# Modulation weights in one float32 product over four column strips, in buffers of their own

## The chip, the cores and the metric

One core of a Trainium2 chip runs the whole program. The metric is the device time of one execution in microseconds, the median of three runs. The core's engines work side by side and meet at semaphores: TensorE (PE, matmuls, and PEld for its weight loads), VectorE (DVE), ScalarE (ACT), GpSimd (POOL), and SyncE (SP), which here does nothing but issue transfers from the chip's memory (HBM) into the on-chip memory (SBUF). Matmul results go to PSUM, eight banks, here held as four pairs `PS[:, pair, half]`.

## The reference, cut to what matters

Two decoder layers run on 512 prompt tokens and 8 sample tokens. Each sub-layer is modulated by nine vectors per layer that come from a conditioning vector `c`, one row for the prompt and one for each of the 8 samples, so 9 rows in all:

```python
mod = jax.nn.silu(c) @ mod_w + mod_b            # (9 rows) x 1024 @ 1024 x 9216
sh0, sc0, gt0, sh1, sc1, gt1, sh2, sc2, gt2 = jnp.split(mod[:, None, :], 9, axis=-1)
h = modulate(rmsnorm(x, norm_pre[0]), sh0, sc0)  # h * (1 + scale) + shift
x = x + 0.5 * gt0 * rmsnorm(swiglu(h, ffn1_in, ffn1_out), norm_post[0])
...                                              # mixing of tokens, with sh1, sc1, gt1
h = modulate(rmsnorm(x, norm_pre[2]), sh2, sc2)
x = x + 0.5 * gt2 * rmsnorm(swiglu(h, ffn2_in, ffn2_out), norm_post[2])
```

`swiglu` multiplies by 1024 x 5632 gate and up weights, then by 2816 x 1024. All data are float32.

## The kernel before, in words

**Weights** come through a ring of four slots, `stage` (512 KB each, 128 x 1024 float32), in one order that is numbered through: a chunk's slot is its number modulo 4. ScalarE rounds a chunk to `w_hi` (L863), VectorE subtracts to get `w_lo` (`lo_apart` or `lo_over`, L1975), and TensorE multiplies `w_hi` and the rest with split activations, `h_hi` and `h_lo`: three products for each block. SP may load a chunk when the one four before it has been split (`lo_done`, L693).

**The gate loop** (`ffn_in`) makes 2 of 22 pairs of gate and up tiles a trip. With m = 0, 1 for the pair and gu = 0, 1 for gate and up, a trip is four tiles of TensorE, each 8 blocks x 3 products x 2 halves of 260 tokens. ScalarE takes `sil` from the gate tile (L949), VectorE multiplies it with the up tile to `hidf` (L2127), ScalarE rounds that to `hid_hi` (L955), VectorE makes `hid_lo`.

**The modulation rows** are a product of 1024 x 9216 a layer, cut into 18 groups of 512 columns. `c_st` holds `silu(c)` transposed, as 9 rounded columns and 9 of the rest; a chunk of weights is the moving operand. Eight groups of layer 0 are made in an opening, ahead of all else (`mod_pair`, 32 chunks, two groups at a time). The other 10, and all 18 of layer 1, are made **beside the gates**: a trip with `group` set has 8 chunks in place of 4, a gate or up chunk and a modulation chunk in turn (`per == 8`), and after each tile TensorE does one modulation chunk (`mod_rows`, 4 matmuls of 512 columns into pair 3). At the next trip, after the first tile, the rows are turned to columns by small matmuls (`turn_rows`), and VectorE adds the bias and writes `modT` (L2109). These trips are in six segments: `f1j0` and `f1i1` in layer 0 (5 trips each), `f2j0` and `f2i1` in layer 0 for layer 1's rows (5 each), and `f1j0` (5) and `f1i1` (3) in layer 1.

**PSUM in such a trip.** Since pair 3 is taken by the modulation rows, the fourth tile (m = gu = 1) goes into pair 0, as the first does:

```python
                                elif m == gu == 0 and per == 8:
                                    if not (type(i) is int and i == 0):
                                        pe.wait_ge(ev_d, i * 2 + ed)
                                    pair = 0
```

`ev_d` counts VectorE's `hidf` products, two a trip, so this wait of the first tile is for all products of the trip before.

Every engine executes its own list in order; a wait holds all that stands behind it on that engine. Nothing reorders the lists: they are as the code writes them.

## Time and profile before

| | |
|---|---|
| median of 3 runs | 3013.66 us (3008.25 to 3019.26) |
| profiled execution, span from first to last instruction | 3023.3 us |
| TensorE busy | 96% of the span |
| VectorE, ScalarE, GpSimd busy | 56%, 39%, 12% |
| mean granted TensorE clock | 0.974 |
| loaded by SP's queue | 296.60 MB |

The page gives the profiled execution by its span alone. Times in rows are microseconds from the span's start. A busy share is an average over stages; which engine sets the pace is read from each stage. A row with x2 or x8 is that many instructions of one kind merged, so its length is from the first one's start to the last one's end; matmuls overlap, so the distance of starts is what one costs. A float32 matmul shows as two records.

### The profile page before, as it was taken

What the parts mean: (1) busy time and instruction counts of PE and PEld (TensorE: products, weight loads), DVE (VectorE), ACT (ScalarE), POOL (GpSimd) and SP (SyncE); (2) the same over time, 40 slices, a digit from 0 to 9 for tenths busy, and PEclk for the clock granted to TensorE, in tenths of its full rate; (3) what the DMA queues carried; (4) which work ended last, traced back from release to release, by engine and by line L of the source; (5) the groups of instructions that cost most, each with busy time, mean ns of one, the idle gap of its engine ahead of it and who ended that gap; (6) DMA issues with size and microseconds to landing.
All of it is one profiled execution on the core that took longest, in us unless ns stands there. A gap on an engine that the chain in (4) does not pass through costs nothing.

```text
span 3023.3 us, 55792 instructions
## 1 busy us (share of the span) xinstructions
PE 2908.2 (96%) x22056; PEld 2703.3 (89%) x22056; DVE 1687.8 (56%) x3427; ACT 1193.3 (39%) x2023; POOL 366.7 (12%) x426
## 2 busy tenths in 40 slices
PE   6999999999999999999999999999999999999998
PEld 5899999899776689999999999999987767999997
DVE  5443346888869475424474424378878775632234
ACT  6533333545444244323334323245453532522222
POOL 2100000324025100000010000011330431100000
PEclk8999999999999999999999999999999999999998
DMA  7443443412224334434434434232222243232321
GB/s 265 127 153 98 141 147 91 137 50 64 57 75 124 107 98 124 145 101 153 124 93 133 141 100 149 86 109 99 57 64 62 62 133 119 85 97 82 100 76 64
DMA packets 448405, 324.28 MB, mean 107 GB/s; under 512 B 25114, under 2 KB 403346, under 8 KB 447451
## 3 DMA queue, kind: packets, MB, share of 16 engines
q1 hardware_dynamic: 442810, 296.60, 32.6%
q0 software_dynamic: 5408, 25.17, 2.5%
q8 instruction: 121, 1.98, 0.3%
q14 instruction: 66, 0.53, 0.1%
HBM read 310.48 MB, written 11.24 MB: 106 GB/s over the span
## 4 chain that ended last, share of the span: by engine, by line
PE 77%; DVE 15%; issue 3%; ACT 2%; DMA 1%; POOL 0%; another core or an unknown queue 0%; ACTq 0%; SPq 0%; DVEq 0%; POOLq 0%
PE PS L1306 77%; DVE score L2514 1%; DVE lo_over L1975 1%; DVE best L2513 1%; DMA stage<-in_mod_w 1%; DVE W L2444 1%; PE PS L1538 1%; DVE score L2504 1%; DVE xT L2071 1%; DMA stage<-in_w_branch_attn 1%; DVE counting L2251 0%; DVE sm L2197 0%; DVE tmpn L2069 0%; DVE lg L2680 0%; DVE dgr L2690 0%
## 5 line engine op out<-in xcount | busy, mean ns | idle before, releaser
L1306 PE MATMUL PS<-h_hi,w_hi 128*128 128x260 f32 (+1 forms) x4000 | 830.4, 289 | 10.5 <-POOL h_lo L2897 5.8
L1306 PE MATMUL PS<-h_lo,w_hi 128*128 128x260 f32 (+1 forms) x4000 | 808.0, 284 | 0.0
L1975 DVE TENSOR_TENSOR lo_apart<-stage,w_hi 128x1024 fp32r<-128x1024 f32 (+2 forms) x448 | 492.9, 1134 | 466.4 <-ACT w_hi L863 462.5
L1306 PEld LDWEIGHTS PS<-h_hi,w_hi 128*128 128x128 f32 (+1 forms) x4000 | 623.4, 189 | 60.5 <-issue 40.3
L1306 PEld LDWEIGHTS PS<-h_lo,w_hi 128*128 128x128 f32 (+1 forms) x4000 | 618.9, 189 | 0.0
L1306 PE MATMUL PS<-h_hi,lo_apart 128*128 128x260 f32 x2816 | 567.2, 283 | 0.0
L863 ACT ACTIVATE w_hi<-stage 128x1024 fp32r<-128x1024 f32 (+3 forms) x586 | 540.9, 954 | 46.8 <-DMA stage<-in_mod_w 15.3
L1306 PEld LDWEIGHTS PS<-h_hi,lo_apart 128*128 128x128 f32 x2816 | 434.6, 189 | 0.0
L1306 PE MATMUL PS<-hid_lo,w_hi 128*128 128x260 f32 x1408 | 283.8, 283 | 0.0
L1306 PE MATMUL PS<-hid_hi,w_hi 128*128 128x260 f32 x1408 | 283.2, 282 | 0.0
L1306 PE MATMUL PS<-hid_hi,lo_apart 128*128 128x260 f32 x1408 | 282.9, 282 | 0.0
L2127 DVE TENSOR_TENSOR hidf<-sil,PS 128x520 f32<-128x520 f32 x88 | 61.3, 697 | 366.5 <-PE PS L1306 366.5
L1306 PE MATMUL PS<-h_hi,lo_over 128*128 128x260 f32 (+1 forms) x1184 | 241.1, 286 | 0.0
L955 ACT ACTIVATE hid_hi<-hidf 128x520 fp32r<-128x520 f32 (+1 forms) x88 | 56.3, 639 | 450.9 <-DVE hidf L2127 450.9
L2878 POOL TENSOR_TENSOR hs<-yT,r_s 128x64 f32<-128x64 f32 x6 | 1.9, 320 | 1853.5 <-ACT r_s L929 1853.5
L1306 PEld LDWEIGHTS PS<-hid_hi,lo_apart 128*128 128x128 f32 x1408 | 217.0, 188 | 0.0
L1306 PEld LDWEIGHTS PS<-hid_hi,w_hi 128*128 128x128 f32 x1408 | 216.8, 188 | 0.1
L1306 PEld LDWEIGHTS PS<-hid_lo,w_hi 128*128 128x128 f32 x1408 | 216.7, 188 | 0.0
L1306 PEld LDWEIGHTS PS<-h_hi,lo_over 128*128 128x128 f32 (+1 forms) x1184 | 184.8, 190 | 0.0
L1975 DVE TENSOR_TENSOR lo_over<-stage,w_hi 128x1024 fp32r<-128x1024 f32 (+1 forms) x138 | 147.2, 1069 | 23.6 <-ACT w_hi L863 22.0
L949 ACT ACTIVATE sil<-PS 128x520 f32<-128x520 f32 x88 | 53.2, 604 | 263.2 <-PE PS L1306 263.2
L1306 PE MATMUL PS<-w_hi,c_st 128*128 128x512 f32 x288 | 116.5, 424 | 11.8 <-DVE lo_apart L1975 11.4
(436 smaller groups left out, 4088.6 us busy)
## 6 DMA issues: line engine op xcount, KB each, us to landing
stage<-in_ffn_in SPq DMA_DIRECT2D x176, 512.0 KB
stage<-in_mod_w SPq DMA_DIRECT2D x144, 512.0 KB
stage<-in_w_in SPq DMA_DIRECT2D x72, 512.0 KB
stage<-in_ffn_out SPq DMA_DIRECT2D x64, 384.0 KB
stage<-in_ffn_out SPq DMA_DIRECT2D x64, 320.0 KB
stage<-in_w_out SPq DMA_DIRECT2D x16, 512.0 KB
x_hold<-xT SPq DMA_DIRECT2D x2, 2080.0 KB
xT<-x_hold SPq DMA_DIRECT2D x2, 2080.0 KB, 8.1
```

Of the source, the lines that this page charges most:

```text
L863: nc.scalar.activation(w_hi[:, ch.slot, 0:ch.elems], stage[:, ch.slot, 0:ch.elems], ACT.Copy)\
L949: nc.scalar.activation(sil[:, m, :].rearrange("p (a n) -> p a n", a=2), PS[:, 2 * m, :, 0:HALF], ACT.Silu).then_inc(ev_a, 1)
L955: nc.scalar.activation(hid_hi[:, bass.ds(i * 2 + (s.first_tile + m), 1), :], hidf[:, m:m + 1, :], ACT.Copy)\
L1306: return nc.tensor.matmul(out, lhsT, rhs, start=start, stop=stop)
L1538: return nc.tensor.transpose(out, in_, ident[p0:p0 + size, p0:p0 + size])
L1975: nc.vector.tensor_tensor(lows(ch)[:, ch.slot, 0:ch.elems], stage[:, ch.slot, 0:ch.elems], w_hi[:, ch.slot, 0:ch.elems].bitcast(FP32), ALU ...
L2071: nc.vector.tensor_tensor(xT[:, k, 0:T], xT[:, k, 0:T], tmpn[:, k % 2, 0:T], ALU.add).then_inc(x_ready, 1)
L2127: nc.vector.tensor_tensor(hidf[:, m, :].rearrange("p (a n) -> p a n", a=2), sil[:, m, :].rearrange("p (a n) -> p a n", a=2), PS[:, up, :, ...
L2444: own(nc.vector.tensor_tensor_scan(W4[:, r, q, 1:NCH + 1], V(6)[:, g:g + 1].to_broadcast([P, NCH]), W4[:, r, q, 1:NCH + 1], 0.0, ALU.mult, ...
L2504: i = nc.vector.scalar_tensor_tensor(sc, rl[:, n % 2, 0:(t + 1) * P], wT[:, t, h:h + 1], sc, ALU.mult, ALU.add)
L2513: own.step(nc.vector.max(best[:], sc))
L2514: own.step(nc.vector.match_replace(sc, best[:], sc, TAKEN))
```

## The change

The modulation weights are no longer split. The whole float32 chunk is the moving operand of a float32 matmul whose stationary operand is `c32`, 32 columns of which 9 are used. A chunk of 1024 columns' worth is cut into four pieces of 256, and the four products go to four strips of 32 partitions of one PSUM bank. The chunks leave the ring: in the opening they go through `mod_open`, 8 slots that lie over `stage` and `w_hi`; beside the gates through four buffers `mod_stage`, one for each quarter of a group. A trip's four modulation chunks are all multiplied at its end, behind the fourth tile. The code can also make two groups a trip (`rate`), but every segment leaves `rate` at 1. ScalarE's list changes with it: what it splits in a trip is the four gate and up chunks alone, in the order of the trips without modulation. `scales` for the first post-norm moves behind the first feed-forward loop.

```diff
-    MOD_FIRST = GROUPS - (FT // 2 - 1)
+    MOD_FIRST = 8
     MOD_PAIRS = MOD_FIRST // 2
-    assert MOD_FIRST == 2 * MOD_PAIRS
+    FIRST_BESIDE = GROUPS - MOD_FIRST
...
-            self.group, self.of_layer, self.mods_before = group, of_layer, mods_before
-            self.per = 4 if group is None else 8
+            self.group, self.of_layer, self.mods_before, self.rate = group, of_layer, mods_before, rate
...
-        return [(s.phase, 4 * s.trips * (s.per // 4), BLK, 2 * s.trips, 2 * s.trips) for s in segments]
+        return [(s.phase, 4 * s.trips, BLK, 2 * s.trips, 2 * s.trips) for s in segments]
...
-    c_st = sb("c_st", [P, KD, P], FP32R)
+    c_st = sb("c_st", [P, 4, P], FP32R)
+    c32 = sb("c32", [P, KD, 32])
...
+    OPEN = 8
+    OPENED = KD * MOD_PAIRS
+    assert OPENED % OPEN == 0
+    mod_open = over("mod_open", [P, OPEN, BLK], ring0)
...
+    MOD_SLOTS = 4
+    mod_at = [arena0 + 2 * TOK * 4 + q * BLK * 4 for q in range(MOD_SLOTS - 1)] + [ffn.at]
+    assert mod_at[-2] + BLK * 4 <= norm_end and ffn.at + BLK * 4 <= nc.sbuf_usable_end
+    mod_stage = [over(f"mod_stage{q}", [P, BLK], at) for q, at in enumerate(mod_at)]
...
-                    for g in range(MOD_PAIRS):
-                        for k in range(4 if g == 0 else 0, KD):
-                            load(chunk('mod', k, g, 8), mod_weights(g, k).unsqueeze(1))
+                    for n in range(4, KD * MOD_PAIRS):
+                        if n >= OPEN:
+                            sp.wait_ge(mod_used, n - OPEN + 1)
+                        sp.dma_start(mod_open[:, n % OPEN, :], mod_weights(n // KD, n % KD)).then_inc(open_full[n % OPEN], 16)
+
+                def mod_load(s, i, m, j):
+
+                    sp.wait_ge(mod_used, i * (4 * s.rate) + (OPENED + 4 * (s.mods_before + m) + j - 3))
+                    sp.dma_start(mod_stage[j][:].rearrange("p (k n) -> p k n", k=2),
+                                 rows_of('mod_w', 2 * j, 2, i * (512 * s.rate) + (s.group + m) * 512, 512, bass.ds(s.of_layer, 1)))\
+                        .then_inc(mod_full[j], 16)
 
                 def ffn_in(s, name, f0):
-                    phase, per = s.phase, s.per
+                    phase = s.phase
 
                     def pair(i):
                         for j in range(4):
-                            load(chunk(phase, j * per // 4, i, per),
+                            load(chunk(phase, j, i, 4),
                                  rows_of(name, 0, KD, (j % 2) * DFF + (f0 + s.first_tile + i * 2 + j // 2) * P, P))
-                            if per == 8:
-                                load(chunk(phase, 2 * j + 1, i, per),
-                                     rows_of('mod_w', 2 * j, 2, i * 512 + s.group * 512, 512, bass.ds(s.of_layer, 1)))
+                            if s.group is not None:
+                                if type(i) is int and i == j == 0 and phase in ('f1j0', 'f2j0'):
+                                    sp.wait_ge(h_lo_ready, (N + (1 if phase == 'f1j0' else 3)) * KD)
+                                if s.rate == 1:
+                                    mod_load(s, i, 0, j)
+                                else:
+                                    mod_load(s, i, j // 2, 2 * (j % 2))
+                                    mod_load(s, i, j // 2, 2 * (j % 2) + 1)
...
                     def body(i):
                         for m in range(2):
-                            at = per // 2 * m
                             if m or split_here(phase, i):
-                                split(chunk(phase, at + 2, i, per))
-                            split(chunk(phase, at + 3, i, per))
-                            act.wait_ge(chunk_used, chunk(phase, at, i, per).number(1))
+                                split(chunk(phase, 2 * m + 2, i, 4))
+                            split(chunk(phase, 2 * m + 3, i, 4))
+                            act.wait_ge(chunk_used, chunk(phase, 2 * m, i, 4).number(1))
                             act.wait_ge(ev_d, i * 2 + (ed + m - 1))
                             nc.scalar.activation(sil[:, m, :].rearrange("p (a n) -> p a n", a=2),
                                                  PS[:, 2 * m, :, 0:HALF], ACT.Silu).then_inc(ev_a, 1)
-                            if per == 8:
-                                split(chunk(phase, at + 4, i, per))
-                                split(chunk(phase, at + 5, i, per))
                             act.wait_ge(ev_d, i * 2 + (ed + m + 1))
                             nc.scalar.activation(hid_hi[:, bass.ds(i * 2 + (s.first_tile + m), 1), :], hidf[:, m:m + 1, :], ACT.Copy)\
                                 .then_inc(hid_hi_ready, 1)
-                        if per == 8:
-                            act.wait_ge(chunk_used, chunk(phase, 7, i, per).number(1))
-                            act.wait_ge(rows_turned, i + (MOD_PAIRS + s.mods_before))
-                            nc.scalar.activation(modrow[:], PS[0:2 * NC, 3, 0, :], ACT.Copy).then_inc(rows_copied, 1)
+                            if s.group is not None and (m == 1 or s.rate == 2):
+                                n = m if s.rate == 2 else 0
+                                act.wait_ge(mod_used, i * (4 * s.rate) + (OPENED + 4 * (s.mods_before + n) + 4))
+                                act.wait_ge(rows_turned, i * s.rate + (MOD_PAIRS + s.mods_before + n))
+                                nc.scalar.activation(modrow[:], PS[:, 3, 0, 0:256], ACT.Copy).then_inc(rows_copied, 1)
...
-                def mod_rows(pair, ch, j):
-
-                    pe.wait_ge(lo_done, ch.number(1))
-                    for k in range(2):
-                        for w in (w_hi, lows(ch)):
-                            last = mm(PS[:, pair, 0, :], c_st[:, 2 * j + k, :], w[:, ch.slot, k * 512:(k + 1) * 512],
-                                      start=(j == 0 and k == 0 and w is w_hi), stop=(j == 3 and k == 1 and w is not w_hi))
-                    last.then_inc(chunk_used, 1)
+                def mod_rows(s, i, m, j):
+
+                    pe.wait_ge(mod_full[j], i * (16 * s.rate) + 16 * (OPENED // OPEN + s.mods_before + m + 1))
+                    for q in range(4):
+                        odd, half = q // 2, q % 2
+                        last = mm(PS[32 * q:32 * q + 32, 3, 0, 0:256], c32[:, 2 * j + odd, :],
+                                  mod_stage[j][:, odd * 512 + half * 256:odd * 512 + half * 256 + 256],
+                                  start=(j == 0), stop=(j == 3))
+                    last.then_inc(mod_used, 1)
 
                 def turn_rows(pair):
 
-                    for q in range(4):
-                        last = mm(PS[:, pair, 1, q * NC:(q + 1) * NC], modrow[:, q * P:(q + 1) * P], sel18[:])
+                    by_block = PS[:, pair, 1, 0:4 * NC].rearrange("p (h q c) -> p q h c", h=2, q=2)
+                    for q in range(2):
+                        last = mm(by_block[:, q], modrow[:, q * P:(q + 1) * P], halves_sel[:].rearrange("p (h c) -> p h c", c=NC))
                     last.then_inc(rows_turned, 1)
...
-                        ch = chunk('mod', k, g, 8)
-                        pe.wait_ge(lo_done, ch.number(1))
+                        n = KD * g + k
+                        pe.wait_ge(open_full[n % OPEN], 16 * (n // OPEN + 1))
                         if k == 0 and g >= 2:
                             pe.wait_ge(ev_a, g - 1)
-                        for w in (w_hi, lows(ch)):
-                            for half in range(2):
-                                last = mm(PS[:, 2 * (g % 2), half, :], c_st[:, k, :], w[:, ch.slot, half * 512:(half + 1) * 512],
-                                          start=(k == 0 and w is w_hi), stop=(k == KD - 1 and w is not w_hi))
-                        last.then_inc(chunk_used, 1)
+                        for q in range(4):
+                            last = mm(PS[32 * q:32 * q + 32, 2 * (g % 2), 0, 0:256], c32[:, k, :],
+                                      mod_open[:, n % OPEN, q * 256:(q + 1) * 256], start=(k == 0), stop=(k == KD - 1))
+                        last.then_inc(mod_used, 1)
...
-                                if m == gu == 0 and per == 8 and not (type(i) is int and i == 0):
-                                    turn_beside(i)
-                                if per == 8:
-                                    mod_rows(3, chunk(phase, 4 * m + 2 * gu + 1, i, per), 2 * m + gu)
+                                if gu == 0 and beside and (m and s.rate == 2 or not m and not (type(i) is int and i == 0)):
+                                    turn_beside(i, m)
+                                if gu == 1 and beside and (m or s.rate == 2):
+                                    for j in range(4):
+                                        mod_rows(s, i, m if s.rate == 2 else 0, j)
...
-                    for k in range(KD):
-                        split(chunk('mod', k + 2, g, 8))
-                        if k == 4 and g:
-                            pair_added(g - 1)
...
-                            at = per // 2 * m
                             if m or split_here(phase, i):
-                                split(chunk(phase, at + 2, i, per))
-                            split(chunk(phase, at + 3, i, per))
-                            if m == 1 and per == 8 and not (type(i) is int and i == 0):
+                                split(chunk(phase, 2 * m + 2, i, 4))
+                            split(chunk(phase, 2 * m + 3, i, 4))
+                            if m == 1 and first_group is not None and not (type(i) is int and i == 0):
                                 rows_beside(i)
                             dve.wait_ge(ev_a, i * 2 + (ea + m + 1))
-                            if per == 8:
-                                split(chunk(phase, at + 4, i, per))
-                                split(chunk(phase, at + 5, i, per))
-                            dve.wait_ge(chunk_used, chunk(phase, at + per // 4, i, per).number(1))
-                            up = 0 if m == 1 and per == 8 else 2 * m + 1
+                            dve.wait_ge(chunk_used, chunk(phase, 2 * m + 1, i, 4).number(1))
+                            up = 0 if m == 1 and first_group is not None else 2 * m + 1
...
```

**SyncE's list**, inside the loop of segment `f1j0` of layer 0, a trip's first three loads. ISA and REGISTER_ALU rows carry the waits in a loop. Before, gate (`in_ffn_in`) and modulation (`in_mod_w`) loads into one ring:

```order
L693 ISA [waits lo_done]
L693 DMA stage<-in_ffn_in 128x8x128
L691 REGISTER_ALU
L693 ISA [waits lo_done]
L693 DMA stage<-in_mod_w 128x2x512
L691 REGISTER_ALU
L693 ISA [waits lo_done]
L693 DMA stage<-in_ffn_in 128x8x128
```

And now:

```order
L714 ISA [waits lo_done]
L714 DMA stage_64<-in_ffn1_in 128x8x128
L726 REGISTER_ALU
L727 ISA [waits mod_used]
L727 DMA mod_stage0_84<-in_mod_w 128x2x512
L710 REGISTER_ALU
L714 ISA [waits lo_done]
L714 DMA stage_64<-in_ffn1_in 128x8x128
```

The modulation load stands where it stood, between two gate loads, but waits for TensorE's use of the buffer (`mod_used`) and no longer for a split.

**ScalarE's list**, same loop, the second half of a trip (m = 1) around `sil`. Before, it splits the fourth gate chunk and the fourth modulation chunk of the trip (slots 2 and 3), does `sil`, and splits the next trip's first two:

```order
L862 REGISTER_ALU [waits stage_full2]
L863 ACTIVATE w_hi<-stage 128x1024 [waits chunk_used]
L862 REGISTER_ALU [waits stage_full3]
L863 ACTIVATE w_hi<-stage 128x1024 [waits chunk_used]
L947 REGISTER_ALU
L948 REGISTER_ALU [waits chunk_used]
L949 ACTIVATE sil<-PS 128x520 [waits ev_d]
L860 REGISTER_ALU
L863 ACTIVATE w_hi<-stage 128x1024 [waits chunk_used,stage_full0]
```

And now, where slots 0 and 1 are gate chunks 0 and 1 of the next trip:

```order
L894 REGISTER_ALU
L899 ACTIVATE w_hi<-stage 128x1024 [waits chunk_used,stage_full0]
L896 REGISTER_ALU [waits stage_full1]
L899 ACTIVATE w_hi<-stage 128x1024 [waits chunk_used]
L980 REGISTER_ALU
L981 REGISTER_ALU [waits chunk_used]
L982 ACTIVATE sil<-PS 128x520 [waits ev_d]
L984 REGISTER_ALU
```

Both splits of the next trip's chunks now stand ahead of `sil`.

**TensorE's list** where one trip of that segment ends and the next begins. Before, the fourth modulation chunk, then the loop and the wait of its first tile:

```order
L1306 MATMUL PS<-w_hi,c_st 128x512 [waits lo_done]
L1306 MATMUL PS<-lo_apart,c_st 128x512
L1306 MATMUL PS<-w_hi,c_st 128x512
L1306 MATMUL PS<-lo_apart,c_st 128x512
L644 UNCONDITIONAL_BRANCH
L644 ISA
L1422 ISA [waits ev_d]
```

And now all four chunks, in strips of 32 partitions:

```order
L1337 MATMUL PS<-mod_stage_84,c 32x256 [waits mod_full0]
L1337 MATMUL PS<-mod_stage_84,c 32x256 x3
L1337 MATMUL PS<-mod_stage_85,c 32x256 [waits mod_full1]
L1337 MATMUL PS<-mod_stage_85,c 32x256 x3
L1337 MATMUL PS<-mod_stage_86,c 32x256 [waits mod_full2]
L1337 MATMUL PS<-mod_stage_86,c 32x256 x3
L1337 MATMUL PS<-mod_stage_87,c 32x256 [waits mod_full3]
L1337 MATMUL PS<-mod_stage_87,c 32x256 x3
L659 UNCONDITIONAL_BRANCH
L659 ISA
L1454 ISA [waits ev_d]
```

The wait for `ev_d` has stayed; 16 strip matmuls stand ahead of it where 4 wide ones stood, and the other 12 wide ones have gone from between the tiles.

## Rows read from the trace of the kernel before

**Rows 1.** The page: the span, and the chain by line.
```profile
span 3023.3 us, 55792 instructions
...
PE PS L1306 77%; DVE score L2514 1%; DVE lo_over L1975 1%; DVE best L2513 1%; DMA stage<-in_mod_w 1%; DVE W L2444 1%; PE PS L1538 1%; DVE score L2504 1%; DVE xT L2071 1%; DMA stage<-in_w_branch_attn 1%; DVE counting L2251 0%; DVE sm L2197 0%; DVE tmpn L2069 0%; DVE lg L2680 0%; DVE dgr L2690 0%
```

**Rows 2.** TensorE in order of time: start, length, line, operation, out<-in.
```profile
121.10 0.39 PE L1306 MATMUL PS<-w_hi,c_st 128*128 128x512 f32 x1
...
122.02 0.40 PE L1306 MATMUL PS<-h_hi,w_hi 128*128 128x260 f32 x2
...
127.78 0.39 PE L1306 MATMUL PS<-w_hi,c_st 128*128 128x512 f32 x1
```

**Rows 3.** TensorE in order of time, at and after a trip's end.
```profile
141.14 0.39 PE L1306 MATMUL PS<-w_hi,c_st 128*128 128x512 f32 x1
...
142.17 0.51 PE L1306 MATMUL PS<-h_hi,w_hi 128*128 128x260 f32 x2
...
148.13 1.05 PE L1306 MATMUL PS<-sel,modrow 18*128 18x9 f32 x8
```

**Rows 4.** One trip: length, busy PE, PEld, DVE, ACT, POOL, clock, DMA.
```profile
142.74:170.85 28.11, 28.11 (x218) 26.97 (x217) 12.44 (x13) 10.55 (x14) 0.00 (x0) 1.00 0.48 149
```

**Rows 5.** The tile modT: minimum, median, maximum in ns.
```profile
L2109 DVE TENSOR_TENSOR modT<-PS,vecT x28: 186/189/197, 160.8 to 1902.3; 128x36 f32 x15, 128x36 f32<-128x36 f32 x13
```

**Rows 6.** VectorE in order of time, same trips.
```profile
122.95 1.23 DVE L1975 TENSOR_TENSOR lo_apart<-stage,w_hi 128x1024 fp32r<-128x1024 f32 x1 [2.64 <-ACT w_hi L863]
...
141.34 0.69 DVE L2127 TENSOR_TENSOR hidf<-sil,PS 128x520 f32<-128x520 f32 x1 [2.66 <-PE PS L1306]
```

**Rows 7.** The opening in order of time, engines mixed; idle time ahead in brackets.
```profile
20.89 47.25 SPq L693 DMA_DIRECT2D stage<-in_mod_w  x28
20.92 1.22 PE L1306 MATMUL PS<-w_hi,c_st 128*128 128x512 f32 x2 [3.64 <-DVE lo_apart L1975]
...
24.44 1.06 ACT L863 ACTIVATE w_hi<-stage 128x1024 fp32r<-128x1024 f32 x1 [1.46 <-DMA stage<-in_mod_w]
...
80.00 1.28 ACT L919 ACT_TABLE_LOAD   x1
...
82.98 0.27 ACT L919 ACTIVATE std<-PS,eps 128x5 f32<-128x5 f32 x1 [1.69 <-PE PS L1306]
...
92.14 0.59 PE L1306 MATMUL PS<-h_hi,w_hi 128*128 128x260 f32 x2
```

**Rows 8.** Two stretches of loads, the columns of rows 4, GB/s last.
```profile
5.00:7.90 2.90, 0.00 (x0) 0.00 (x0) 0.00 (x0) 0.00 (x0) 2.06 (x8) 1.00 1.02 414
...
72.00:80.00 8.00, 6.20 (x24) 4.69 (x23) 5.05 (x5) 5.55 (x6) 1.82 (x1) 0.78 0.96 281
```

**Rows 9.** TensorE in order of time, float32 of 512 columns.
```profile
1014.19 3.60 PE L1306 MATMUL PS<-kv,Exd 128*64 128x512 f32 x8
1017.72 0.39 PE L1306 MATMUL PS<-y_hi,w_hi 128*128 128x260 f32 x1
```

**Rows 10.** TensorE in order of time, float32 in strips of 32 columns.
```profile
724.80 0.39 PE L1306 MATMUL PS<-h_hi,lo_over 128*128 128x260 f32 x2
725.12 0.67 PE L1306 MATMUL PS<-CA,BXl 128*32 128x128 f32 x16
725.72 0.50 PE L1306 MATMUL PS<-h_hi,w_hi 128*128 128x260 f32 x2
```

**Rows 11.** A gate load's issue, and the split that uses it.
```profile
70.27 0.38 SPq L693 DMA_DIRECT2D stage<-in_ffn_in  x1
...
75.58 1.06 ACT L863 ACTIVATE w_hi<-stage 128x1024 fp32r<-128x1024 f32 x1 [1.43 <-DMA stage<-in_ffn_in]
```

**Rows 12.** Stretches after TensorE has waited, the columns of rows 4.
```profile
20.90:24.30 3.40, 3.38 (x8) 2.71 (x9) 3.37 (x3) 2.08 (x3) 1.26 (x1) 0.50 0.68 206
...
2613.10:2618.40 5.30, 5.30 (x16) 4.43 (x17) 5.13 (x8) 3.94 (x6) 3.52 (x3) 0.50 0.00 0
```

More of the change, by code:

```diff
@@ L64, in arrivals @@
     def arrivals(self):
-        n = 16 * (self.base // 4 + 1)
+        n = 16 * (self.base // 4 + 1) + self.before
         return n if self.shift is None else self.shift * 4 + n
@@ L450, in build @@
     vec_in = sem("vec_in")
+    mod_full = [sem(f"mod_full{q}") for q in range(MOD_SLOTS)]
+    mod_used = sem("mod_used")
+    open_full = stage_full + mod_full
     def mod_weights(g, k):
@@ L481, in _ @@
         def _(pool):
-            own = Chain(pool, pool_own)
+            own = Chain(pool, pool_step)
             def pick_where(t, value, pattern, base, mult, op, fill):
@@ L493, in _ @@
             pick_where(ident[:], ident[:], [[-1, P]], 0, 1, ALU.not_equal, 1.0)
[L494 to L495 removed]
+            by_half = halves_sel[:].rearrange("p (h c) -> p h c", c=NC)
+            for odd in range(2):
+                pick_where(by_half, by_half, [[-32, 2], [-1, NC]], -64 * odd, 1, ALU.not_equal, 1.0)
             by_sample = samesample[:].rearrange("p (b g) -> p b g", g=NPG)
@@ L515, in _ @@
             pool.memset(r_s[:], 1.0).then_inc(consts_ready, 1)
+            own.wait()
+            steps_taken['pool'] = own.n
         @block.scalar
@@ L540, in _ @@
                                            ident[0:NC, 0:NC])
-            last.then_inc(c_turned, 1)
+            last.then_inc(x_turned, 1)
         @block.vector
         def _(dve):
-            own = Chain(dve, dve_own0)
+            own = Chain(dve, dve_own)
             dve.wait_ge(consts_ready, 1)
@@ L1332, in pair_turned @@
                         pe.wait_ge(ev_d, g - 1)
-                    for q in range(8):
-                        last = mm(PS[:, 1, g % 2, q * NC:(q + 1) * NC], modrows[:, q // 4, q % 4 * P:(q % 4 + 1) * P], sel18[:])
+                    for q in range(2):
+                        last = nc.tensor.transpose(PS[:, 1, g % 2, q * P:(q + 1) * P], modrows[:, g % 2, q * P:(q + 1) * P], ident[:])
                     last.then_inc(rows_turned, 1)
@@ L1442, in ffn_in @@
                 def ffn_in(s, j=None):
-                    phase, per = s.phase, s.per
+                    phase, beside = s.phase, s.group is not None
                     ea, ed = evicts_a[phase], evicts_d[phase]
@@ L1460, in body @@
                     def body(i, h_waits=None):
-                        if h_waits is not None and per == 4:
-                            tiles_together((0, 1, 2), [chunk(phase, q, i, per) for q in range(3)], (h_hi, h_lo), h_waits)
+                        if h_waits is not None:
+                            tiles_together((0, 1, 2), [chunk(phase, q, i, 4) for q in range(3)], (h_hi, h_lo), h_waits)
                         for m in range(2):
                             for gu in range(2):
-                                if h_waits is not None and per == 4 and 2 * m + gu < 3:
+                                if h_waits is not None and 2 * m + gu < 3:
                                     continue
-                                if m == gu == 1 and per == 8:
+                                if m == gu == 1 and beside:
                                     pe.wait_ge(ev_a, i * 2 + (ea + 1))
                                     pair = 0
-                                elif m == gu == 0 and per == 8:
+                                elif m == gu == 0 and beside:
                                     if not (type(i) is int and i == 0):
@@ L1480, in body @@
                                         pe.wait_ge(mod_added, mods_added(l))
-                                tile(pair, [(chunk(phase, (2 * m + gu) * per // 4, i, per), 0, KD, P)], (h_hi, h_lo),
+                                tile(pair, [(chunk(phase, 2 * m + gu, i, 4), 0, KD, P)], (h_hi, h_lo),
                                      h_waits=h_waits if m == gu == 0 else None)
@@ L1497, in ffn_in @@
                     each(pe, s.trips, trip, last=False)
-                    if per == 8:
+                    if beside:
                         turn_beside(s.trips)
@@ L1982, in pair_added, with scales @@
                     dve.wait_ge(rows_turned, g + 1)
[L1983 to L1994 removed]
+                    bias = vecT[:, 48 + 8 * g:56 + 8 * g].rearrange("p (j q) -> p q j", q=2)
+                    nc.vector.tensor_tensor(modT[:, 8 * g:8 * g + 8, :].rearrange("p (j q) c -> p q j c", q=2),
+                                            PS[:, 1, g % 2, 0:2 * P].rearrange("p (q j c) -> p q j c", q=2, j=4)[:, :, :, 0:NC],
+                                            bias.unsqueeze(3).to_broadcast([P, 2, 4, NC]), ALU.add).then_inc(ev_d, 1)
+                def scales(j, pre=True, post=True):
                     def blocks(which):
@@ L2134, in body @@
                                                     ALU.subtract).then_inc(hid_lo_ready, 1)
+                            if m == 1 and first_group is not None and s.rate == 2:
+                                rows_beside(i, 1)
                     each(dve, s.trips, body)
-                    if per == 8:
+                    if first_group is not None:
                         rows_beside(s.trips)
```

128 lines of the change are left out of this document (63 added, 65 removed).

## Prediction

> **What bounds the kernel now.** I read the page first: of a span of 3023.3 us the chain that ended last runs over TensorE's matmuls for 77% [rows 1]. A microsecond counts if TensorE works or stands in it.
>
> Next, TensorE in order of time inside a trip of the gate loop. A modulation chunk is four matmuls from 121.10 to 122.02, 0.92 us. The next stands at 127.78, 6.68 us after the first, so a gate or up tile takes 6.68 - 0.92 = 5.76 us (48 matmuls at 0.12), with no gap [rows 2]. A trip is four tiles and four chunks, 26.72 us, and the turn of the finished rows, which begins at 148.13 [rows 3]. Together it is 28.11 us: in the stretch 142.74 to 170.85, from one trip to the same place of the next, PE is busy for all of it at a granted clock of 1.00, VectorE for 12.44 and ScalarE for 10.55 us [rows 4]. In these loops only TensorE's work counts. There are 28 such trips (the sum for `modT` is made 28 times, rows 5), in segments of 5, 5, 5, 5, 5 and 3.
>
> The seam between trips needs care. The last tile of a trip goes into PSUM pair 0, and so does the first of the next, so TensorE must wait until VectorE has taken the product `hidf` out. Now that product starts at 141.34 and takes 0.69 us [rows 6] while TensorE is covered by the fourth modulation chunk, begun at 141.14; the next tile starts at 142.17, 1.03 us after the old one's end [rows 3].
>
> Last, the opening. TensorE waits for splits, these for transfers, and the first gate matmul is at 92.14. The 28 loads issued from 20.89 on take 47.25 us, 1.69 each [rows 7]; with nothing holding the queue back, 4 KB rows move at 414 GB/s (1.27 us a chunk of 512 KB), gate chunks at 281 (1.87 us) [rows 8].
>
> **The change, part by part.**
>
> *Matmuls beside the gates.* Removed: 4 chunks x 0.92 = 3.68 us a trip. Added: 16 products of 256 columns in float32. What float32 costs: eight records of 512 columns (four matmuls, two passes each) begin at 1014.19, and the next matmul at 1017.72, 0.43 us a record counting a step of shape [rows 9]; so 256 columns are 0.215 us a pass. Whether four column strips run at once: sixteen records of 128 columns, in strips of 32, occupy 725.12 to 725.72, 0.60 us; one after the other, at a quarter of 0.43, they would take 1.7. From the last full-width matmul (0.12 after 724.80) to the next full-width one it is 0.80 us; four rounds of 0.108 and a step of 0.12 leave 0.25 us for going in and out [rows 10]. So a trip's product is 4 chunks x 2 passes x 0.215 + 0.25 = 1.97 us; without overlap, its upper bound, 32 x 0.215 = 6.9 us.
> The Trainium skill (TensorEngine Tiling, Key Properties) says that changing the tiling mode drains TensorE. By that rule the trace's 0.25 us is paid at each change of shape, and the new code, with a trip's four chunks together, pays it once.
>
> *Turning the rows.* Now 8 records in 1.05 us [rows 3], some 0.11 us each; then 4: -0.45 us a trip.
>
> *The splits.* Four copies and four subtractions a trip vanish from ScalarE and VectorE. They lie under TensorE's work [rows 4]: no gain in itself.
>
> *The loads, and the new wait.* SP serves its list in order. Each modulation load now waits until TensorE has used the same buffer a trip earlier, and all four uses stand at the trip's end. Modulation load 0 stands ahead of gate chunk 1, so gate chunk 1 of trip i+1 is not asked for before TensorE has done all four tiles and the first modulation chunk of trip i. ScalarE, in the second half of trip i, splits gate chunks 0 and 1 of trip i+1 and only then does `sil` of that half; before, what stood ahead of `sil` had long been asked for. `hidf` waits for `sil`, and the next first tile for `hidf`. So **TensorE stands at each seam for a whole load.** Worked out from the last tile's end (141.14 in the old trip):
> - change of shape 0.12, first chunk 0.43, its end and the signal 0.15: SP is free at 0.70. Modulation load 0 leaves at 0.80, gate chunk 1 one issue later, 1.25.
> - the transfer: a gate chunk issued at 70.27 with another ahead of it is first used at 75.58, 5.3 us [rows 11]; so here at 6.55. Bounds from its issue: one chunk at 414 and one at 281 GB/s with some 0.5 us of start, 3.6; with one more of 1.87 sharing the queue and as much again for its neighbour, 7.
> - ScalarE's split 1.06 [rows 11]: 7.61. VectorE's split 1.23, the sum for `modT` 0.19 and the product 0.69 [rows 5, 6], with `sil` beside them: 9.72. TensorE starts 0.14 later, as now: 9.9 us against 1.03.
>
> TensorE's own 1.97 us lie inside these 9.9, so at such a seam the cheaper product gains nothing; TensorE is idle for 7.9 us. Late behind it is everything of the next trip, but once: chunks 2 and 3 have a tile or more to land.
>
> *The clock.* After a TensorE gap of 3.64 us (20.92, rows 7) the granted clock is 0.50, 1.2 GHz, over 20.90 to 24.30. In the second layer a stretch of 5.30 us with TensorE busy throughout, just after a wait for h_lo, is at 0.50 too [rows 12]. Half speed for 3.4 us loses about 1.5 us of matmul work (a little less than half of it), for 5.3 us 2.4. I take 1.5, the row whose gap I know, with 0 and 2.4 as bounds.
> The Trainium skill (TensorE: Matmul & The Clock Gate, "HAM oscillation — how this bites in real kernels") warns of this pattern, a loop that waits for data between bursts. By it every seam pays; without it the sum would be 33 us less.
>
> *How many seams.* The wait bites between trips of one segment: 4+4+4+4+4+2 = 22. In a segment's first trip the buffers have long been free, and after its last come loads with no such wait. Per seam +8.9 (9.9 - 1.03), -2.76 (the other three chunks), -0.45, +1.5 = +7.2; x22 = **+158 us**. The 6 last trips: -3.68 + 1.97 - 0.45 = -2.16; x6 = **-13 us**.
>
> *The opening.* The 28 loads now leave without splits, eight buffers deep. The first is used 3.5 us after its issue (20.89, 24.44, rows 7); issued at some 18.6: 22.1; 27 more at 1.27: 56.4. Gate chunk 2 lands at 56.4 + 3 x 1.87 = 62.0; split, table load and `std` (1.06, 1.28, 0.27) end at 64.7, where now they end at 83.25; the rest, 8.9 us to the first gate matmul, stays [rows 7]. So 73.6 for 92.14: **-18.5 us** (-12 if a chunk takes 1.5 us).
>
> Sum: +158 - 13 - 18.5 = +126.5 on the profiled 3023.3, so 3150. That execution is 9.6 us above the median of the three timed ones, 3013.66; set on the median, **3140 us**.
>
> **The rivals.**
> - *The seam is hidden.* Were gate chunk 1 there in time, each trip would gain 2.16: 28 x 2.16 + 18.5 = 79, **2935 us**. All else in the change shortens work. It decides at (13 + 18.5)/22 = 1.4 us net a seam, against 7.2: the chunk would have to land 5.8 us earlier, before it is asked for. What remains is that I misread what a wait counts. 0.08.
> - *The seam is cheaper.* Landing after 3.6 and no loss by the clock: 22 x 3.2 less, **3070 us**. The gap of 3.64 us that did lower the clock speaks against the second half. 0.12.
> - *The seam is dearer.* The queue, asked for eight chunks in a burst, lands chunk 1 after 7 us and the clock costs 2.4: 22 x 2.6 more, **3197 us**. 0.10.
> - *The strips do not overlap in this form.* The first chunk is then 1.3 us later at each seam (28 us), the last trips cost 6 x 4.9 and the opening some 12: **3209 us**. The sixteen records in 0.60 us speak against it. 0.05.
> - *Seam and gains cancel* within 0.3% (9 us, about what a measurement of this kernel can tell). It needs 1.0 to 1.8 us net a seam. 0.02.
> - The forecast, 3100 to 3175: 0.63.
>
> **How the numbers follow.** Slower by over 0.3% are the forecast, the cheap and the dear seam and the strips, 0.90; same 0.02; faster 0.08. The range, 3075 to 3190, takes in most of the cheap and the dear seam's cases and leaves out the hidden one and the separate strips.
>
> **What the profile after would show.** A TensorE gap of 7 to 8 us ahead of a first tile in 22 places, the matmuls behind it at clock 0.50; 28 bursts of 32 records in about 2 us; `sil` held up by a split that waits for a transfer; the issue of gate chunk 1 right behind the first modulation chunk's use; trips of some 35 us; the first gate matmul near 74. I am wrong if the seams are under 3 us, or if the strips' records come 0.2 us apart.

## The result

| | before | after |
|---|---|---|
| median | 3016.32 us (3008.25 to 3019.26, 4 runs) | 3153.97 us (3147.07 to 3165.95, 4 runs) |
| profiled execution, span | 3023.3 us | 3145.3 us |
| TensorE busy, mean granted clock | 96%, 0.974 | 91%, 0.949 |

The ratio is 1.047, 95% interval 1.044 to 1.050: the change makes the kernel 138 us slower by the medians. I predicted 3140 us, slower, with a range of 3075 to 3190.

**The page** of after, its span, its chain by line, and the group of the gate tiles' first product (count | busy us, mean ns | idle time ahead and what ended it), answers to [rows 1]:

```profile
span 3145.3 us, 56068 instructions
...
PE PS L1337 71%; DMA stage<-in_ffn_in 4%; DVE score L2542 1%; DVE lo_over L2008 1%; DVE best L2541 1%; DMA mod_open<-in_mod_w 1%; ACT w_hi L899 1%; DVE W L2472 1%; DVE score L2532 1%; DMA stage<-in_w_branch_attn 1%; DVE xT L2099 1%; DVE counting L2279 1%; PE PS L1571 0%; DMA stage<-in_w_in 0%; DVE tmpn L2097 0%
...
L1337 PE MATMUL PS<-h_hi,w_hi 128*128 128x260 f32 (+1 forms) x4000 | 851.4, 295 | 182.4 <-DVE hidf L2151 171.9
```

A transfer that is not among the chain's parts shown in [rows 1], the gate weights', is on it now with 4%, and TensorE's tiles stand 171.9 us waiting for `hidf`. The view of waits (us in total, times, longest) counts how often:

```profile
PE PS L1337 <- DVE hidf L2151: 171.9, 22, 9.0
...
SPq L727 <- PE PS L1337: 584.8, 22, 28.8
```

22 waits of TensorE, one for each place where two trips of a segment meet, and 22 waits of SP's queue at the modulation load (L727) for TensorE. The same number on both sides fits one cause but does not show it: e1 and e2 below keep the 22 waits of the queue (429.3 and 443.9 us in all) and lose TensorE's. One seam in order of time, TensorE first (start, length, then the idle time ahead in brackets):

```profile
228.53 0.41 PE L1337 MATMUL PS<-h_hi,lo_apart 128*128 128x260 f32 x2
228.87 1.93 PE L1337 MATMUL PS<-mod_stage,c 128*32 128x256 f32 x32
238.50 0.80 PE L1337 MATMUL PS<-h_hi,w_hi 128*128 128x260 f32 x2 [7.70 <-DVE hidf L2151]
```

SP's queue:

```profile
229.72 0.37 SPq L727 DMA_DIRECT2D mod_stage<-in_mod_w  x1
230.34 0.37 SPq L714 DMA_DIRECT2D stage<-in_ffn_in  x1
```

ScalarE and then VectorE:

```profile
235.34 1.06 ACT L899 ACTIVATE w_hi<-stage 128x1024 fp32r<-128x1024 f32 x1 [15.48 <-DMA stage<-in_ffn_in]
236.31 0.58 ACT L982 ACTIVATE sil<-PS 128x520 f32<-128x520 f32 x1
```
```profile
236.43 1.23 DVE L2008 TENSOR_TENSOR lo_apart<-stage,w_hi 128x1024 fp32r<-128x1024 f32 x1 [15.31 <-ACT w_hi L899]
237.57 0.19 DVE L2137 TENSOR_TENSOR modT<-PS,vecT 128x36 f32 x1
237.68 0.69 DVE L2151 TENSOR_TENSOR hidf<-sil,PS 128x520 f32<-128x520 f32 x1
```

Read it from the end. The tile at 238.50 follows the end of `hidf`. VectorE started `hidf` at 237.68, as soon as it had done the split of 236.43 and the small sum for `modT`. That split waited for ScalarE's, and ScalarE had waited 15.48 us for a transfer, the one issued at 230.34, right behind a modulation load that could go only when TensorE had used the first chunk of its burst. Before, the same seam took 1.03 us [rows 3].

What follows the seam is slow too. Windows of after (length, then busy time of PE, PEld, DVE, ACT and POOL, granted clock, DMA share, GB/s):

```profile
228.85:238.50 9.65, 1.95 (x34) 0.94 (x33) 1.94 (x3) 1.55 (x2) 0.00 (x0) 0.79 0.84 248
238.50:241.90 3.40, 3.40 (x15) 3.40 (x16) 1.93 (x2) 1.85 (x3) 0.00 (x0) 0.50 1.10 335
241.90:244.70 2.80, 2.80 (x15) 2.80 (x14) 1.23 (x1) 1.06 (x1) 0.00 (x0) 0.51 1.14 311
```

TensorE is busy throughout the second and third, but at a granted clock of 0.50 and 0.51, 1.2 GHz. By the Trainium skill (TensorE: Matmul & The Clock Gate, "HAM oscillation — how this bites in real kernels") a loop that waits for data between bursts pays so each time round; the trace agrees, in all 22 places.

From turn to turn of the rows, a trip with a seam in it now takes 35.42 us on the mean of 16, where it took 28.11 [rows 4]: +7.31. The last trips' interval takes 20.50 where it took 23.23: -2.73.

**The opening** got shorter. TensorE, ScalarE and TensorE again:

```profile
26.65 0.64 PE L1337 MATMUL PS<-mod_open,c 128*32 128x256 f32 x8 [0.64 <-DMA mod_open<-in_mod_w]
29.48 1.02 PE L1337 MATMUL PS<-mod_open,c 128*32 128x256 f32 x8 [2.19 <-DMA mod_open<-in_mod_w]
...
59.01 0.64 PE L1337 MATMUL PS<-mod_open,c 128*32 128x256 f32 x8 [0.72 <-DMA mod_open<-in_mod_w]
```
```profile
64.25 1.06 ACT L899 ACTIVATE w_hi<-stage 128x1024 fp32r<-128x1024 f32 x1 [0.68 <-DMA stage<-in_ffn_in]
...
66.62 0.27 ACT L953 ACTIVATE std<-PS,eps 128x5 f32<-128x5 f32 x1
```
```profile
75.78 0.64 PE L1337 MATMUL PS<-h_hi,w_hi 128*128 128x260 f32 x2
```

The first gate matmul is at 75.78 where it was at 92.14 [rows 7]: -16.4. In sum: 22 x 7.31 = +160.8, 6 x -2.73 = -16.4, the opening -16.4: +128.0. The two spans differ by +122.0. The other 6 us lie outside these trips: between the last turn of layer 0's second segment and the first of its third it is 726.37 us where it was 722.97, though it holds a seam of +7.31, so 3.9 less; behind the last turn of all the stretch is 3.8 shorter; from layer 0's last turn to layer 1's first it is 2.4 more than a seam accounts for. The same kernel run again takes 730.52 in the first of these stretches, 4.1 more than here, so differences of this size need no cause in the code.

### The profile page after: what moved, and what is told of

Same layout as the page of the kernel before. It is cut to its first block, busy times and chain, and to the rows that moved or that the text cites. A ratio compares the mean times of both kernels' runs of the same rounds, so it can differ in the third digit from the quotient of the medians.

```text
span 3145.3 us, 56068 instructions
## 1 busy us (share of the span) xinstructions
PE 2855.1 (91%) x22464; PEld 2647.6 (84%) x22464; DVE 1516.8 (48%) x3282; ACT 1047.4 (33%) x1879; POOL 360.4 (11%) x427
## 4 chain that ended last, share of the span: by engine, by line
PE 72%; DVE 15%; DMA 6%; issue 3%; ACT 3%; SPq 0%; POOL 0%; DVEq 0%; another core or an unknown queue 0%; ACTq 0%; POOLq 0%
PE PS L1337 71%; DMA stage<-in_ffn_in 4%; DVE score L2542 1%; DVE lo_over L2008 1%; DVE best L2541 1%; DMA mod_open<-in_mod_w 1%; ACT w_hi L899 1%; DVE W L2472 1%; DVE score L2532 1%; DMA stage<-in_w_branch_attn 1%; DVE xT L2099 1%; DVE counting L2279 1%; PE PS L1571 0%; DMA stage<-in_w_in 0%; DVE tmpn L2097 0%
## 5 line engine op out<-in xcount | busy, mean ns | idle before, releaser
L1337 PE MATMUL PS<-h_hi,w_hi 128*128 128x260 f32 (+1 forms) x4000 | 851.4, 295 | 182.4 <-DVE hidf L2151 171.9
L1337 PEld LDWEIGHTS PS<-h_hi,w_hi 128*128 128x128 f32 (+1 forms) x4000 | 635.7, 195 | 226.8 <-DVE lo_apart L2008 182.1
L1337 PE MATMUL PS<-h_lo,w_hi 128*128 128x260 f32 (+1 forms) x4000 | 823.0, 288 | 0.0
L1337 PEld LDWEIGHTS PS<-h_lo,w_hi 128*128 128x128 f32 (+1 forms) x4000 | 635.8, 194 | 0.0
L2008 DVE TENSOR_TENSOR lo_apart<-stage,w_hi 128x1024 fp32r<-128x1024 f32 (+2 forms) x304 | 321.5, 1085 | 625.5 <-ACT w_hi L899 621.9
L1337 PE MATMUL PS<-h_hi,lo_apart 128*128 128x260 f32 x2816 | 581.8, 289 | 0.0
L899 ACT ACTIVATE w_hi<-stage 128x1024 fp32r<-128x1024 f32 (+4 forms) x442 | 398.0, 923 | 407.3 <-DMA stage<-in_ffn_in 384.0
L1337 PEld LDWEIGHTS PS<-h_hi,lo_apart 128*128 128x128 f32 x2816 | 449.7, 195 | 0.0
L2157 DVE TENSOR_TENSOR hid_lo<-hidf,hid_hi 128x520 fp32r<-128x520 f32 (+1 forms) x88 | 61.6, 700 | 75.2 <-ACT hid_hi L985 75.2
```

Of the source, the lines that this page charges most:

```text
L899: nc.scalar.activation(w_hi[:, ch.slot, 0:ch.elems], stage[:, ch.slot, 0:ch.elems], ACT.Copy)\
L1337: return nc.tensor.matmul(out, lhsT, rhs, start=start, stop=stop)
L2008: nc.vector.tensor_tensor(lows(ch)[:, ch.slot, 0:ch.elems], stage[:, ch.slot, 0:ch.elems], w_hi[:, ch.slot, 0:ch.elems].bitcast(FP32), ALU ...
L2157: nc.vector.tensor_tensor(hid_lo[:, f, :], hidf[:, m:m + 1, :], hid_hi[:, f, :].bitcast(FP32), ALU.subtract).then_inc(hid_lo_ready, 1)
```

## The experiments

The kernels were timed in two sets, each beside the kernel before: e1 to e4 in the first, where that kernel's median was 3018.36 us, and e5 to e9 in the second, where it was 3015.20. The changed kernel, run again in the second set (**e9_after_again**), stands for the first set's as well.

> The changed kernel itself, unchanged, beside the others of this set, to put the prices of the filler and of the second load ahead on a firm base. 3154 again within 10 us; its profile shows 22 TensorE gaps of 7.5 to 9 us as before.

3148.35 us (3143.27 to 3158.73), ratio 1.044 (1.041 to 1.046); 22 waits of 175.5 us in all. The price of the change is 133 to 138 us.

### e1_swap: three loads moved by one place each

```diff
 for j in range(4):
     load(chunk(phase, j, i, 4),
...
-    if s.group is not None:
...
+    if s.group is not None and j > 0:
...
         if s.rate == 1:
-            mod_load(s, i, 0, j)
+            mod_load(s, i, 0, j - 1)
+            if j == 3:
+                mod_load(s, i, 0, 3)
```

Modulation loads 0, 1 and 2 each go behind one more gate load; load 3 stays last. Gate chunk 1 now has no modulation load ahead of it. The wait for `h_lo` that two segments have in their first trip moves with load 0.

> Each modulation load is issued one gate chunk later, so that gate chunk 1 of a trip no longer has one ahead of it. Theory (the seam is gate chunk 1's issue time and nothing else): all 22 TensorE gaps of 7.5 to 9 us go, a trip lasts 25.4 us from turn to turn, and the clock loss behind the gaps goes too; 28 x 2.7 + 16.4 = 93 us less than the kernel before's 3016, about 2925. Rival (the memory queue or the splits' own rate holds the chunk, not its place): gaps stay above 3 us, 3050 or more. Second rival (gate chunk 2, which now stands behind the wait, becomes the late one): a gap ahead of the second gate tile, over 2 us.

2928.92 us (2921.98 to 2937.82), ratio 0.971 (0.967 to 0.974): 219 to 225 us faster than the changed kernel, and faster than before. TensorE at the seam, and a window of one trip:

```profile
197.59 1.93 PE L1339 MATMUL PS<-mod_stage,c 128*32 128x256 f32 x32
199.46 0.51 PE L1339 MATMUL PS<-h_hi,w_hi 128*128 128x260 f32 x2
```
```profile
171.90:197.47 25.57, 25.57 (x230) 24.50 (x228) 7.71 (x9) 6.78 (x9) 0.00 (x0) 1.00 0.56 164
```

No gap is left and no half speed; every trip takes 25.57 us. The rival of a limit by the queue's or the splits' rate falls: the same bytes are loaded and split. So does the one of gate chunk 2 as the next late one. As this trip has no wait, it also prices the new work: from the last gate matmul to the next tile's first it is 2.08 us, of which 0.12 is a gate matmul, so a burst costs 1.96 us.

### e2_sil_first: the late chunk left late, sil ahead of its split

```diff
-split(chunk(phase, 2 * m + 3, i, 4))
+late = m == 1 and s.group is not None
+if not late:
+    split(chunk(phase, 2 * m + 3, i, 4))
...
 nc.scalar.activation(sil[:, m, :].rearrange("p (a n) -> p a n", a=2),
                      PS[:, 2 * m, :, 0:HALF], ACT.Silu).then_inc(ev_a, 1)
+if late:
+    split(chunk(phase, 2 * m + 3, i, 4))
```

VectorE's list has the same edit, with its split behind `hidf`.

> The loads keep their order, so gate chunk 1 is asked for as late as in the changed kernel; ScalarE and VectorE do sil and hidf of the trip's second half before they split that chunk. Theory (the first tile waits only because sil stands behind the split): the first tile starts some 1.6 to 2.2 us after the last one's end; the chunk is low and ready at 8.9, the second tile could start at about 8.4, so a wait of 0.5 to 1 us moves to there; about 2940. Rival (the late chunk costs its lateness wherever it is waited for): the gap of 7 us moves to the second tile, 3150.

2955.27 us (2952.16 to 2963.66), ratio 0.979 (0.976 to 0.982). The gap at the first tile is gone though the transfer comes as late as before, so what TensorE waited for was the order of ScalarE's and VectorE's lists. A trip takes 26.69 us on the mean, 1.1 more than in e1, and the rest sits behind the first tile, as expected. ScalarE, VectorE and TensorE in a trip whose seam is at 206:

```profile
211.23 1.06 ACT L899 ACTIVATE w_hi<-stage 128x1024 fp32r<-128x1024 f32 x1 [11.70 <-DMA stage<-in_ffn_in]
212.19 0.62 ACT L989 ACTIVATE hid_hi<-hidf 128x520 f32 x1
212.72 0.36 ACT L995 ACTIVATE modrow<-PS 128x256 f32<-128x256 f32 x1
```
```profile
212.32 1.23 DVE L2012 TENSOR_TENSOR lo_apart<-stage,w_hi 128x1024 fp32r<-128x1024 f32 x1 [6.95 <-ACT w_hi L899]
```
```profile
213.23 0.59 PE L1341 MATMUL PS<-halves_sel,modrow 128*128 128x18 f32 x4 [0.83 <-ACT modrow L995]
213.67 0.49 PE L1341 MATMUL PS<-h_hi,w_hi 128*128 128x260 f32 x2
```

The wait shows at the turn of the rows, ahead of the second tile, because the copy to `modrow` stands behind the late split: 14.0 us in 18 places. But the second tile had to wait for the chunk as well, as I expected. Its subtraction ends at 213.55 and the tile starts at 213.67, 0.12 us later; in the 22 trips that distance is 0.07 to 0.29 us. So the turn's wait lies inside the chunk's, and a copy that came sooner would have gained next to nothing. In the trip of 27.26 us the chunk's split began some 0.7 us later than in the others. In the two longest, 27.84 and 27.94 us, TensorE ran at half speed for 3.4 us, soon after waits of 1.45 and 1.55 us.

### e3_filler: the gap filled with useless matmuls

```diff
 if not (type(i) is int and i == 0):
+    pe.wait_ge(ev_d, i * 2 + (ed - 1))
+    kept_running(PS[:, 1, 0, :], 34)
     pe.wait_ge(ev_d, i * 2 + ed)
```

> The changed kernel with 34 matmuls of 512 columns of no use in each of the 22 gaps, into a free PSUM pair, before the wait for hidf. They take some 7.3 us of the 7.8 us gap. Theory (about 2 us of a seam's price is the lowered clock behind the gap): the granted clock stays at 1.00 across the seam, the first tile takes 5.7 us for 7.67, and the time falls by 22 x 2.0 = 44 us to about 3110. Rival (the first tile is long for another reason, such as the chunk's arrival): no change, 3154. If the filler runs past the gap, up to 22 x 0.5 us is added.

3098.16 us (3087.94 to 3110.21), ratio 1.025 (1.022 to 1.029), 50 to 56 us less than the changed kernel, with 748 more matmuls. Windows over a seam (the first from the burst to the next tile) and over that tile:

```profile
220.76:230.47 9.71, 9.71 (x68) 7.29 (x67) 1.93 (x3) 1.59 (x3) 0.00 (x0) 1.00 0.87 250
230.47:236.22 5.75, 5.75 (x49) 5.75 (x49) 3.15 (x3) 2.88 (x4) 0.00 (x0) 1.00 1.12 325
```

The seam is as long as ever, but the clock stays at 1.00, 2.4 GHz, and the first tile takes 5.75 us. In the changed kernel it takes 7.2 to 8.6 us in the 22 places, 7.8 on the mean. A trip takes 33.44 us, 2.0 less. 22 x 2.0 = 44 us is the clock's share. That is in keeping with the timed difference: beside the changed kernel of the other set, the ratios are 0.018 apart with some 0.004 of uncertainty, 43 to 67 us.

### e4_spread: strips, but one chunk behind each tile

```diff
-if gu == 1 and beside and (m or s.rate == 2):
-    for j in range(4):
-        mod_rows(s, i, m if s.rate == 2 else 0, j)
+if beside:
+    mod_rows(s, i, 0, 2 * m + gu)
```

> The modulation chunks in strips as in the changed kernel, but one behind each tile, where they stood before, the loads in the changed order. Modulation buffer 0 is then free after the first tile of a trip, three tiles earlier. Theory: no gap at the seam, since gate chunk 1 is asked for three tiles earlier; a trip pays the change of shape four times, 4 x (0.43 + 0.25) + 23.04 + 0.52 = 26.3 us for 28.11 before; 28 x 1.8 + 16.4 = 67 us less than before, about 2950. Rival (buffers of their own and not the burst at the end make the seam): gaps of over 5 us stay, 3100 or more.

2969.30 us (2961.34 to 2974.52), ratio 0.984 (0.981 to 0.987). The load order is that of the changed kernel and no long gap is left: the first modulation buffer is free three tiles earlier. So buffers of their own and the loads' order are not enough for a seam; it needs the burst at the trip's end as well. A trip takes 26.92 us where I had 26.3. Two chunks in order of time, the second at a trip's end:

```profile
198.90 0.64 PE L1337 MATMUL PS<-mod_stage,c 128*32 128x256 f32 x8
199.47 0.51 PE L1337 MATMUL PS<-h_hi,w_hi 128*128 128x260 f32 x2
...
205.43 0.64 PE L1337 MATMUL PS<-mod_stage,c 128*32 128x256 f32 x8
206.44 0.51 PE L1337 MATMUL PS<-h_hi,w_hi 128*128 128x260 f32 x2 [0.36 <-DVE hidf L2150]
```

The second is 1.01 us ahead of the next tile where the first is 0.57: one chunk is no longer enough to cover `hidf`. That is 0.44 of the 0.6 us by which the trip is longer than I had it; the rest I did not follow.

### e5_serial: e1's loads, all products in one column strip

```diff
-last = mm(PS[32 * q:32 * q + 32, 3, 0, 0:256], c32[:, 2 * j + odd, :],
+last = mm(PS[0:32, 3, 0, 0:256], c32[:, 2 * j + odd, :],
           mod_stage[j][:, odd * 512 + half * 256:odd * 512 + half * 256 + 256],
-          start=(j == 0), stop=(j == 3))
+          start=(j == q == 0), stop=(j == q == 3))
```

The opening's matmuls are changed in the same way.

> e1's order of loads, and all four products of a modulation chunk in column strip 0, one on top of the other (the rows come out wrong: the sum of four quarters), so that no two can run at once; the number of matmuls and their columns stay. Theory (four strips run at once, a round of four 256-column passes in 0.215 us): the burst of 32 records grows from 1.56 to some 6.7 us from first to last start, a trip from 25.57 to 30.7 us, the opening from 1.28 to 1.72 us a chunk; 28 x 5.1 + 14 = 157 us more than e1's 2929, about 3085. Rival (the strips gain little, the saving is that a product in float32 needs no second operand): burst unchanged within 1 us, 2930 to 2960.

3091.60 us (3087.57 to 3095.81), ratio 1.025 (1.023 to 1.027), 160 us more than e7, its neighbour in the set. TensorE:

```profile
361.11 7.09 PE L1339 MATMUL PS<-mod_stage,c 128*32 128x256 f32 x32
368.13 0.51 PE L1339 MATMUL PS<-h_hi,w_hi 128*128 128x260 f32 x2
```

The same 32 records now take 6.71 us from the first start to the last, for 1.55: a pass of 256 columns costs 6.71 / 31 = 0.22 us alone, and four in four strips cost 1.55 / 7 = 0.22 us together. A trip takes 30.73 us, and 28 x 5.16 = 144 us of the 160 are there, the rest in the opening (first gate matmul at 91.61 for 75.34 in e7). In float32 on one strip the product is dearer than the split one it replaced; all of its gain is the four strips.

### e8_two_ahead: one modulation load more ahead of gate chunks 1, 2 and 3

```diff
-    mod_load(s, i, 0, j)
+    for q in ((0, 1), (2,), (3,), ())[j]:
+        mod_load(s, i, 0, q)
```

> The changed kernel with two modulation loads ahead of gate chunk 1 of each trip, so that this chunk waits for the second modulation chunk's use and has one load more ahead of it in the queue. Theory (the seam is set by when gate chunk 1 lands): it is asked for 0.6 us later and lands 0.6 to 1.9 us later; seams of 10.6 to 11.9 us for 9.96, 22 x that difference = 13 to 41 us more than the changed kernel, 3167 to 3195. Rival (the seam is a fixed cost of meeting at pair 0, whatever the loads do): seams of 9.96 and no change.

3195.51 us (3193.60 to 3199.94), ratio 1.060 (1.059 to 1.062): 47 us more than the changed kernel beside it, a little over the range I gave. SP's queue and ScalarE, at a seam whose last gate matmul starts at 367.36:

```profile
368.55 1.01 SPq L727 DMA_DIRECT2D mod_stage<-in_mod_w  x2
369.81 0.37 SPq L714 DMA_DIRECT2D stage<-in_ffn_in  x1
```
```profile
375.69 1.06 ACT L900 ACTIVATE w_hi<-stage 128x1024 fp32r<-128x1024 f32 x1 [17.02 <-DMA stage<-in_ffn_in]
```

From issue to split it is now 5.9 us, where it was 5.0 (230.34 to 235.34): a load ahead costs its issue, 0.6, and here 0.9 more behind it in the queue. The seams are 11.92 us on the mean, 1.8 to 2.0 more than the changed kernel's. The seam is no fixed price of meeting at pair 0.

### e7_both: both cures

The edits of e1 and e2 together.

> Both cures together: each modulation load one gate chunk later (e1), and sil and hidf of a trip's second half ahead of the split of the next gate chunk (e2). Theory (with the chunk there in time, nothing waits for the splits either): trips of 25.57 us as in e1, the same time as e1 within the measurement, about 2929. Rival (the splits held sil up by a little in every trip, seen or not): seams under 2.08 us and up to 22 x 0.3 = 7 us less.

2931.17 us (2919.50 to 2939.16), ratio 0.972 (0.969 to 0.975): the same as e1, trips of 25.57 us. Either cure removes the seam; where the loads are in order, that of the lists brings nothing. The version that beats both kernels is e1.

## Why the prediction was right, and where its sizes were off

**Sign and mechanism** were right: "TensorE stands at each seam for a whole load". It is shown by e1 and e8, which change only the places of modulation loads in SP's list and take the seam away or lengthen it, and by e2, which leaves the load late and takes the wait for it out of `hidf`'s way.

**The seam.** Predicted 9.9 us from the last tile's end; measured 9.96 from the start of its last matmul, so 9.84. Its stations, from that end (228.77, 0.12 after the last gate matmul of the trip shown; forecast in brackets): modulation load 0.95 (0.80), gate chunk 1 issued 1.57 (1.25), ScalarE's split 6.57 (6.55), `hidf` from 8.91 (9.03 in the same sum), tile 9.73 (9.9). The transfer was 0.3 us shorter than the 5.3 of [rows 11] and the issues 0.3 later, which cancelled: that part of the agreement is luck.

**The clock** was the mis-sized term: 1.5 us a seam from [rows 12], 2.0 measured (the first tile takes 7.8 us on the mean for 5.75) and 2.0 by e3's trips. I took the half speed to last 3.4 us; it lies over 3.0 to 6.2 us of the first tile, 4.4 on the mean, and the seam shown above is one of the longest. Over 22 seams that is some 11 us more than forecast.

**The sum** hides it. It was forecast at +126.5 and came to +128.0 by the same terms: a seam's trip cost 7.31 for the 7.2 forecast, because the turn and the chunks that went gave back most of what the clock took more. So the clock is not why 3140 was 14 us low. The medians lie 137.7 us apart, 11 more than forecast, and the spans of the two profiled executions 122.0: the one before (3023.3) was longer than all four timed ones (3008.25 to 3019.26), the one after the shortest of its four. The other 2.7 us of the 14 are what the median before rose by with a fourth run.

**The new work** was right: 1.97 us a burst, measured 1.96, overlap and mode change included. By the Trainium skill (TensorEngine Tiling, Key Properties) a change of mode drains the array; e1 shows its size here, 1.96 - 8 x 0.215 = 0.24 us for going in and out.

**The turn** gave more than the 0.45 us I took: the next matmul stands 0.37 us behind its start (179.75, 180.12 in e1) for 0.99 before (148.13, 149.12), and the chunk behind it, which cost 1.03 and not 0.92, went too. With the 0.11 us more that the chunk at the seam cost, e1's trip comes out: -3.68 + 1.96 - 0.62 - 0.11 - 0.11 = -2.56, measured -2.54. The last trips' -2.73 for -2.16 has the same cause in the main.

**The opening** gave 16.4 us for 18.5. The chunks came every 1.28 us as forecast, but for one pause (26.65 to 29.48, some 1.5 us more), and the last was used at 59.0; the rest of the chain stayed as it was, as assumed (9.16 us from `std` to the first gate matmul in both). The term varies from run to run: in the profiles of the experiments, e5's aside, the first gate matmul is at 74.10 to 76.01.

**The rivals.** "The strips do not overlap" is refuted by e5. "The seam is hidden" did not happen, but its 2935 us is about what e1 reached (2929) by the places of three loads: the gain was real, and it was in the new work, not in the order around it. "Dearer" is about what e8 made, 3196 for 3197 us, though with a transfer of 5.9 us where that rival had 7: the agreement of the two times is partly chance. That taking away the splits gains nothing in itself I read from [rows 4] and did not try.

## What to carry to other kernels

Ask of each wait in a queue what stands behind it, not what it guards: here the wait for a buffer whose data was not needed before the next trip's end held up a load that was needed at once. When uses are gathered into a burst, their buffers come free in a burst too, and late; then put the loads for them behind those that are wanted sooner. A gap on TensorE can cost more than its length: here 2.0 us of lost speed on top of 7.8 us of idling.

## What the runs showed of the hardware

- Four float32 products of 256 columns in four column strips took the time of one, 0.22 us a pass; in one strip each took its own (e5 against e1).
- The half speed after the gaps of 7.5 to 9.0 us lay over 3.0 to 6.2 us of the tile behind, from seam to seam; after the gap of 3.64 us in [rows 7, 12] it lasted 3.4. The length of the one gap just before does not settle whether the clock falls. After a gap of 2.12 us in e2 it stayed at 1.00 over the next 6.8 us, and after one of 1.45 us it fell (TensorE, then windows):

```profile
1157.02 0.59 PE L1341 MATMUL PS<-halves_sel,modrow 128*128 128x18 f32 x4 [2.12 <-ACT vecT L998]
```
```profile
158.74 0.59 PE L1341 MATMUL PS<-halves_sel,modrow 128*128 128x18 f32 x4 [1.45 <-ACT modrow L995]
```
```profile
158.74:162.14 3.40, 3.40 (x19) 3.40 (x20) 2.09 (x3) 1.06 (x1) 0.00 (x0) 0.63 1.10 333
```
```profile
1157.10:1160.50 3.40, 3.40 (x29) 3.40 (x30) 1.91 (x3) 1.06 (x1) 0.00 (x0) 1.00 1.10 338
1160.50:1163.90 3.40, 3.40 (x30) 3.40 (x29) 1.58 (x2) 1.55 (x2) 0.00 (x0) 1.00 0.65 178
```

- The opening's loads, rows of 4 KB, ran at 404 GB/s over 28.5 us, with TensorE idle a third of the time; the window of that stretch:

```profile
29.48:58.00 28.52, 19.08 (x190) 4.47 (x190) 0.70 (x3) 2.87 (x6) 6.56 (x6) 0.82 1.03 404
```
